# A two-layer encoder trunk on one core: attention's values one unit behind its scores, its products spread evenly, and loads and weights brought a stage forward

## The chip, the cores and the metric

The kernel runs on one core of a Trainium2 chip. The metric is the device time of one execution in microseconds, from the launch's first to its last instruction; lower is better. The core's engines run their own instruction streams and meet at semaphores: TensorE (PE, matmul; PEld is its weight load), VectorE (DVE), ScalarE (ACT), GpSimd (POOL) and SyncE (SP), which issues all DMAs of this kernel.

## What is computed

`encoder_trunk` is applied with the same weights to a prompt of 2048 rows and a sample of 512 rows, 1024 wide, all in float32. It has two layers; the first is the one that the change touches:

```python
h = rmsnorm(x, ln_g[0])
q_lat, kv_lat, k_pe, q_mem, gate = split(h @ w_in_a)          # 384, 256, 32, 256, 1024
q = rmsnorm((rmsnorm(q_lat) @ w_uq).reshape(S, 12, 96));  q = rope(q)
k_nope, v = split((rmsnorm(kv_lat) @ w_ukv).reshape(S, 12, 128))
k = rope(rmsnorm(concat(k_nope, k_pe)))                       # 12 heads of 96
o_mix = softmax(q @ k.T * 96 ** -0.5) @ v                     # prompt and sample each among themselves
x = x + (concat(o_mix, o_mem) * silu(gate)) @ w_out[0]        # o_mem: attention over 256 memory rows
```

The second layer has a spatial gating unit in attention's place.

## The kernel before

Rows are handled as 20 tiles of 128 (16 of the prompt, 4 of the sample). Every matmul operand is split into a high and a low part (`hi`, `lo`) in TensorE's reduced float32 form, and each product is three matmuls: hi x hi, hi x lo, lo x hi (lines 169 to 173). The high part is a copy by ScalarE, the low part a subtraction by VectorE. The stages run one after another, each in a block of its own. The exit of a space that owns semaphores (line 58) clears them and sets a barrier for all engines.

**Latents** (`latents`, line 312). Steps 0 to 20. A step normalizes and transposes the next row tile (`NormTranspose`: `square` on ScalarE, `root` on GpSimd, `scale` on VectorE, `turn` on TensorE, `round_hi`, `take_lo`), makes the 48 matmuls of the latents of this tile (`products`), and turns, splits and stores the latents of the tile before. In steps 2, 4, ... 16 a tile of memory rows is turned as well, in the middle of the products, its two halves at k = 2 and k = 5 (line 379). A turn waits until the low half of the transposition before has been taken. x tiles have two buffers. The order of each engine's work in a step is written out by hand (lines 354, 398, 433, 451, 491).

**Weights** (`Weights`, line 123, `Plan`, line 92). Raw weights go through a buffer of 6144 columns; ScalarE copies the high and VectorE subtracts the low part. A stage's first pieces are loaded by the stage before (`load_following`). The heads have five pieces, three of 1152 columns and two of 1536; four fit, and the fifth is loaded in the heads' stage.

**Heads** (`heads`, line 509). Per tile: queries (27 matmuls of 384 columns) and keys with values (18 of 512) from the latents, norms, rotary positions (tables made by GpSimd at the start, lines 753 to 769), transpositions of keys two tiles behind (`turn_k`) and of queries one tile behind (`turn_q`), splits and stores to `qT`, `kT`, `vS`. SP's order per step is written at lines 592 to 604: values, keys of two tiles behind, latents two ahead, queries of one behind. The stage waits for all stores before it ends. On VectorE `value_lo` stands before the three `low_k` (lines 881 to 884).

**Attention** (`attention`, line 955). 12 heads x 5 chunks of 512 queries: parts 0 to 3 of the prompt with 8 units of 256 keys each, and the sample with 2. A unit is: `scores` (6 matmuls of 512 columns into one of two PSUM buffers), two exponentials by ScalarE (lines 1203, 1204; the first is the high part of the probabilities), the low part by VectorE (line 1311), `value` (4 matmuls). GpSimd adds up the high parts (line 1277), so that the row sums need no matmul: per chunk 7 additions, then `fold`, `total_lo` and, of the outputs, `join`. `total` (2 matmuls) brings the sums into `o_lo`. The maximum over the keys is taken 22 pieces ahead: `maximum` (2 matmuls a unit), a reduction of each piece by VectorE (line 1297), and behind a chunk's last piece the reduction to one value per row and its negation `neg` (line 1305). This falls behind the fifth unit (t = 4) of parts 0, 1 and 2 and behind the seventh (t = 6) of parts 2 and 3. Four small DMAs (`row`, line 1048) write it as the bias row of the queries, for which the first scores of the next chunk wait. Scores of unit t + 1 wait for the low part of unit t - 1. TensorE's order is:

```python
for t in range(c.pairs):
    if t < c.pairs - 1:
        scores(c, t + 1)
    maximum(*max_pieces(c, t))
    if nxt.exists() and t == c.pairs - 1:
        scores(nxt, 0)
    if t == 0 and has_before(c):
        finish_values(prev)          # the last two units of the chunk before
    if t >= 2:
        value(c, t - 2)
    if t == 3 and has_before(c):
        total(prev)
```

GpSimd's order in a chunk of 8 is fold (of the chunk before), additions 1 and 2, total_lo, addition 3, join, additions 4 to 7. At the stage's start SP loads queries 0, keys 0, queries 1 and values 0; VectorE sets the constant rows (lines 1318 to 1322), for which `maximum` waits too; then come 22 pieces of maxima and the first scores.

After attention come `gate_memory`, `gated_output`, and `spatial` with the same two for layer 1 (`build`, line 2211).

## Time and profile before

| | us |
|---|---|
| median of 3 runs (3455.32 to 3460.83) | 3456.26 |
| the profiled execution | 3457.05 |
| its span, first to last instruction | 3455.3 |
| PE busy | 3244.4 (94%) |
| PE weight loads busy | 2752.9 (80%) |
| DVE busy | 2024.7 (59%) |
| ACT busy | 1707.5 (49%) |
| POOL busy | 1398.5 (40%) |

The profile is of one execution; times count from the span's start. The granted clock is a share of full speed (1.00 is 2.4 GHz, 0.50 is 1.2 GHz); its mean over the span is 0.969. "busy" is the time in which at least one instruction of the engine runs; matmuls are pipelined and overlap in the records (one of 512 columns lasts 0.39 to 0.40 us and the next starts 0.23 us later), so a TensorE that is 99% busy need not be at its peak: the distance of the starts shows it. In a timeline row the first number is the start, the second the duration, "xN" the number of merged instructions, and the bracket the idle time of the engine before them and who ended it. In a row of waits stand who waited for whom, then us in total, times, and the longest.

### The profile page before, as it was taken

What the parts mean: (1) busy time and instruction counts of PE and PEld (TensorE: products, weight loads), DVE (VectorE), ACT (ScalarE), POOL (GpSimd) and SP (SyncE); (2) the same over time, 40 slices, a digit from 0 to 9 for tenths busy, and PEclk for the clock granted to TensorE, in tenths of its full rate; (3) what the DMA queues carried; (4) which work ended last, traced back from release to release, by engine and by line L of the source; (5) the groups of instructions that cost most, each with busy time, mean ns of one, the idle gap of its engine ahead of it and who ended that gap; (6) DMA issues with size and microseconds to landing.
All of it is one profiled execution on the core that took longest, in us unless ns stands there. A gap on an engine that the chain in (4) does not pass through costs nothing. (4 is left out here: it accounts for less than half of the span.)

```text
span 3455.3 us, 46901 instructions
## 1 busy us (share of the span) xinstructions
PE 3244.4 (94%) x17548; PEld 2752.9 (80%) x17548; DVE 2024.7 (59%) x2857; ACT 1707.5 (49%) x2472; POOL 1398.5 (40%) x910
## 2 busy tenths in 40 slices
PE   7979979999999999999979997998999979999899
PEld 6978856777777777777769997786788869999787
DVE  4548878888888888888753333444333234333432
ACT  4436645777777777777744544102222225444200
POOL 1228856888888888888910000000110000000000
PEclk9989979999999999999989998998999989999999
DMA  7858983333213333321053233885323233322565
GB/s 285 307 211 311 328 281 73 63 68 64 50 41 63 68 65 68 64 59 36 11 200 110 89 111 89 243 229 185 140 97 108 81 144 126 107 91 85 165 192 157
DMA packets 380229, 454.75 MB, mean 132 GB/s; under 512 B 51704, under 2 KB 317304, under 8 KB 367728
## 3 DMA queue, kind: packets, MB, share of 16 engines
q1 hardware_dynamic: 380016, 451.91, 42.5%
q8 instruction: 134, 2.20, 0.3%
q14 instruction: 79, 0.65, 0.1%
HBM read 262.07 MB, written 189.64 MB: 131 GB/s over the span
## 5 line engine op out<-in xcount | busy, mean ns | idle before, releaser
L1277 POOL TENSOR_TENSOR at_acc<-at_acc,at_ph 128x1024 f32<-128x1024 f32 x288 | 690.6, 2398 | 76.1 <-ACT at_ph L1203 55.7
L1203 ACT ACTIVATE at_ph<-at_sc 128x1024 fp32r<-128x1024 f32 x408 | 418.5, 1026 | 322.8 <-PE at_sc L1123 322.8
L1311 DVE TENSOR_TENSOR at_pl<-at_sc,at_ph 128x1024 fp32r<-128x1024 f32 x408 | 498.5, 1222 | 129.7 <-ACT at_sc L1204 129.3
L1297 DVE TENSOR_REDUCE at_mx<-at_mxp 128x1 f32<-128x512 f32 x816 | 522.1, 681 | 25.8 <-PE at_mxp L1134 23.8
L1204 ACT ACTIVATE at_sc<-at_sc 128x1024 f32<-128x1024 f32 x408 | 416.0, 1020 | 0.0
L171 PE MATMUL gm_gate<-gm_h,gm_g_hi 128*128 128x256 f32 x1280 | 367.7, 287 | 6.4 <-DVE gm_g_lo L160 6.4
L172 PE MATMUL gm_gate<-gm_h,gm_g_hi 128*128 128x256 f32 x1280 | 362.1, 283 | 0.0
L173 PE MATMUL gm_gate<-gm_h,gm_g_lo 128*128 128x256 f32 x1280 | 361.9, 283 | 0.0
L1119 PE MATMUL at_sc<-at_qt,at_kt 97*128 97x512 f32 x816 | 330.5, 405 | 3.9 <-DVE at_pl L1311 1.9
L1121 PE MATMUL at_sc<-at_qt,at_kt 96*128 96x512 f32 x816 | 325.0, 398 | 0.0
L1148 PE MATMUL at_o_hi<-at_ph,at_v 128*128 128x512 f32 x816 | 322.3, 395 | 2.1 <-DVE at_half L1316 2.1
L1123 PE MATMUL at_sc<-at_qt,at_kt 96*128 96x512 f32 x816 | 322.5, 395 | 0.0
L1150 PE MATMUL at_o_lo<-at_pl,at_v 128*97 128x512 f32 x816 | 321.9, 395 | 0.0
L1134 PE MATMUL at_mxp<-at_kt,at_qt 96*128 96x512 f32 x816 | 275.7, 410 | 22.7 <-DMA at_kt<-kT 17.9
L171 PE MATMUL ou_acc<-ou_o_hi,ou_og 128*128 128x512 f32 x640 | 252.4, 394 | 43.1 <-DVE ou_o_lo L160 35.3
L1632 POOL TENSOR_TENSOR gm_rstd<-gm_mean,all_mhalf 128x4 f32<-128x4 f32 x40 | 40.3, 1007 | 618.7 <-DVE gm_mean L1772 618.7
L172 PE MATMUL ou_acc<-ou_o_lo,ou_og 128*128 128x512 f32 x640 | 251.6, 393 | 0.0
L173 PE MATMUL ou_acc<-ou_o_hi,ou_og 128*128 128x512 f32 x640 | 251.2, 393 | 0.0
L171 PEld LDWEIGHTS gm_gate<-gm_h,gm_g_hi 128*128 128x128 f32 x1280 | 245.1, 192 | 6.8 <-DVE gm_g_lo L160 6.8
L172 PEld LDWEIGHTS gm_gate<-gm_h,gm_g_hi 128*128 128x128 f32 x1280 | 245.6, 192 | 0.0
L173 PEld LDWEIGHTS gm_gate<-gm_h,gm_g_lo 128*128 128x128 f32 x1280 | 245.3, 192 | 0.0
L1919 ACT CAST ou_og<-ou_full 128x1024 fp32r<-128x1024 f32 x40 | 42.0, 1049 | 392.2 <-DVE ou_full L1938 392.2
(240 smaller groups left out, 7297.1 us busy)
## 6 DMA issues: line engine op xcount, KB each, us to landing
gm_h<-hT SPq DMA_DIRECT2D x48, 1024.0 KB, 7.2
hT<-lat_n_h SPq DMA_DIRECT2D x28, 1024.0 KB, 7.2
qT<-hd_stq SPq DMA_DIRECT2D x60, 384.0 KB, 5.4
kT<-hd_stk SPq DMA_DIRECT2D x60, 384.0 KB, 4.7
at_qt<-qT SPq DMA_DIRECT2D x120, 192.0 KB, 3.0
sgT<-gm_sg SPq DMA_DIRECT2D x80, 256.0 KB, 2.1
ou_o<-omix SPq DMA_DIRECT2D x40, 512.0 KB, 6.3
ou_sg<-sgT SPq DMA_DIRECT2D x40, 512.0 KB, 7.4
```

The source lines that it names most:

```text
L171: pe.matmul(out, a_hi, w_hi, start=first, stop=False)
L172: pe.matmul(out, a_hi, w_lo, start=False, stop=False)
L173: return pe.matmul(out, a_lo, w_hi, start=False, stop=last)
L1119: pe.matmul(sc[g][:, b, :], kt[:, c.kv, 0, ks], qt[:, c.quad, 0, :], start=True, stop=False)
L1121: pe.matmul(sc[g][:, b, :], kt[0:QK, c.kv, 0, ks], qt[0:QK, c.quad, 1, :], start=False, stop=False)
L1123: m = pe.matmul(sc[g][:, b, :], kt[0:QK, c.kv, 1, ks], qt[0:QK, c.quad, 0, :], start=False, stop=True)
L1148: pe.matmul(o_hi[:], v[:, c.kv, n, 0:2 * VH], ph[:, g, b, :], start=first and b == 0, stop=last and b == 1)
L1203: act.activation(ph[:, g], sc[g % 2][:], ACT.Exp, scale=SCALE).then_inc(p_hi, 1)
L1204: act.activation(sc[g % 2][:], sc[g % 2][:], ACT.Exp, scale=SCALE).then_inc(p_in, 1)
L1277: pool.tensor_tensor(acc[:, c.slot, :], f32(ph[:, (g - 1) % 4]).rearrange("p b n -> p (b n)") if t == 1 else acc[:, c.slot, :], now, ALU.a ...
L1297: dve.tensor_reduce(mx[:, n:n + 1], mxp[n % 2][:], AX.X, ALU.max).then_inc(mx_in, 1)
L1311: dve.tensor_tensor(pl[:, g], sc[g % 2][:], f32(ph[:, g]), ALU.subtract).then_inc(p_lo, 1)
```

## The change

It moves work between stages and changes orders; what is computed stays the same.

- Attention, TensorE: every unit is now scores, maximum, values; the first scores of the next chunk stand ahead of the last maxima. Values run one unit behind; the last unit's values of a chunk follow in the next chunk's first step, values 0 and 1 both at t = 2. `total` moves from t = 3 to t = 1 (t = 2 behind a sample chunk), starts the accumulation in `o_lo`, and waits for the copy `low` of the chunk before.
- Attention, ScalarE: `total_hi` one or two steps earlier, before exponentials 1; `low` is copied before `up`. GpSimd: `total_lo` before addition 1 (before addition 2 behind a sample chunk).
- Latents: only the first gains are loaded first, the others after tile 0; the turns of the memory tile move from k = 2 and 5 to k = 3 and 6; ScalarE rounds before it squares; in steps 2 to 6 one piece of the heads' weights is split per step; the fifth piece is loaded in step 5, the following stage's six in step 13, the first two latent tiles in step 16.
- Heads: all weights are there at the start; the first low key part is taken before the values'; in the drain, between the stores of the last queries and of the last keys, queries 0, keys 0 (16 tiles) and queries 1 of attention are loaded, and the sample's keys 0 after the waits for all stores.
- `build`: the spaces for the above, with semaphores of their own. The keys' buffer is split into two tensors, so the constants have one more instruction.

```diff
+        self.gains_in = [s.sem(f"n_gains{n}") for n in range(2)]
...
-    def load_gains(self, sp):
-        for tile, rows in zip(self.g, self.gains):
-            sp.dma_start(tile[:], rows.broadcast_to([P, D])).then_inc(self.g_in, 16)
+    def load_gains(self, sp, others):
+        for n in range(1, len(self.g)) if others else (0,):
+            sp.dma_start(self.g[n][:], self.gains[n].broadcast_to([P, D])).then_inc(self.gains_in[others], 16)
...
+        if self.order[n][2] > 0:
+            dve.wait_ge(self.gains_in[1], 16 * (len(self.gains) - 1))
...
+class HeadsAhead:
+
+
+    STEPS = 5
+
+    def __init__(self, s, plan, following):
+        self.w = Weights(s, plan, following)
+        self.lat = s.sb("lat", [P, 2, 2, QL + KVL], F32R)
+        self.lat_in = [s.sem(f"lat{u}") for u in range(2)]
+
+    def load(self, sp, u, rows):
+        sp.dma_start(f32(self.lat[:, u]), rows).then_inc(self.lat_in[u], 16)
+
+
+class KeysAhead:
+
+
+    def __init__(self, s):
+        self.k0 = s.sb("k0", [QK + 1, 2, TOK], F32R)
+        self.q = s.sb("q", [QK + 1, 4, 2, BLK], F32R)
+        self.q_load = [s.sem(f"q_load{u}") for u in range(4)]
+        self.kh_load = [s.sem(f"kh_load{u}") for u in range(2)]
+        self.kl_load = [s.sem(f"kl_load{u}") for u in range(2)]
+
+    def load_q(self, sp, qT, head, part, quad):
+        for a in range(2):
+            sp.dma_start(f32(self.q[0:QK, quad, a]).rearrange("d (t n) -> d t n", n=P),
+                         qT[part * 4:(part + 1) * 4, head // 4, :, head % 4, a].rearrange("t d n -> d t n")
+                         ).then_inc(self.q_load[quad], 16)
+
+    def load_first(self, sp, kT, a, b):
+
+        for n, sem in ((0, self.kh_load[0]), (1, self.kl_load[0])):
+            sp.dma_start(f32(self.k0[0:QK, n, a * P:b * P]).rearrange("d (t n) -> d t n", n=P),
+                         kT[a:b, 0, 0:QK, n, 0].rearrange("t p n -> p t n")).then_inc(sem, 16)
...
+                norm.load_gains(sp, 1)
                 w.load(sp)
 
                 def step(i):
+                    if i == 5:
+                        ahead.w.load_rest(sp)
+                    if i == 13:
+                        ahead.w.load_following(sp)
...
+                    if i == 16:
+                        for u in range(2):
+                            sp.wait_ge(stored[u], 16)
+                            ahead.load(sp, u, latT[u])
...
-                        if beside and k in (2, 5):
-                            norm.turn(pe, beside[0], k // 5)
+                        if beside and k in (3, 6):
+                            norm.turn(pe, beside[0], k // 6)
...
+                    turned = list(norm.between(i, i + 1))
+                    for n in turned[:1]:
+                        for half in range(2):
+                            norm.round_hi(act, n, half)
                     for n in norm.between(i + 1, i + 2):
                         norm.square(act, n)
-                    for n in norm.between(i, i + 1):
+                    for n in turned[1:]:
                         for half in range(2):
                             norm.round_hi(act, n, half)
                     if here(i):
                         square(i)
                     if here(i - 1):
                         round_hi(i - 1)
+                    if 2 <= i < 2 + ahead.STEPS:
+                        ahead.w.round_hi(act, i - 2, i - 1)
 
...
+                    if 2 <= i < 2 + ahead.STEPS:
+                        ahead.w.take_lo(dve, i - 2, i - 1)
...
-        w = Weights(s, plan, following)
-        lat = s.sb("lat", [P, 2, 2, QL + KVL], F32R)
+        w, lat, lat_in = ahead.w, ahead.lat, ahead.lat_in
...
-                load_lat(Tile(0, 0))
...
-                load_lat(Tile(0, 1))
-                w.load(sp)
...
+                    if t.known and t.n == TILES:
+                        sp.wait_ge(q_st[0], 16 * PT_TILES)
+                        keys.load_q(sp, qT, 0, 0, 0)
+                        sp.wait_ge(k_st[0], 16 * PT_TILES)
+                        keys.load_first(sp, kT, 0, PT_TILES)
+                        keys.load_q(sp, qT, 0, 1, 1)
...
+                keys.load_first(sp, kT, PT_TILES, TILES)
 
             @block.tensor
             def _(pe):
+                w.ready(pe, "ukv", 1)
...
                         key_mean(t1)
+                    if t2.within(TILES):
+                        low_k(t2, 0)
+                    if t1.within(TILES):
                         value_lo(t1)
                     if t2.within(TILES):
-                        for c in range(G):
-                            low_k(t2, c)
+                        low_k(t2, 1)
+                        low_k(t2, 2)
...
-        kt = s.sb("kt", [QK + 1, 2, 2, TOK], F32R)
-        qt = s.sb("qt", [QK + 1, 4, 2, BLK], F32R)
+        kt, qt = (keys.k0, s.sb("k1", [QK + 1, 2, TOK], F32R)), keys.q
...
+            first = 16 if c.head % 2 == 0 and c.n > 0 else 0
+            return first + 16 * sum(len(list(key_pieces(n))) for n in range(c.head % 2, c.head + 1, 2))
...
+        def total_at(c):
+
+            return 2 if before(c, 1).sample else 1
...
                 c0 = Chunk(0)
-                load_q(c0)
-                load_k(0)
-                load_q(c0.ahead(1))
                 load_v(0)
-                sp.wait_ge(const_in, 5)
+                sp.wait_ge(const_in, 6)
                 row(c0)
...
-                        if c.part == 0:
+                        if c.part == 0 or c.n == Chunk.PARTS - 1:
                             pe.wait_ge(kl_load[c.kv], keys_loaded(c))
...
-                                      start=first and b == 0, stop=last and b == 1)
+                                      start=first and b == 0 and not has_before(c), stop=last and b == 1)
                     m.then_inc(valued, 1)
 
                 def total(c, alone=False):
 
                     pe.wait_ge(tot_lo_in, c.n + 1)
+                    pe.wait_ge(low_in, c.n + 1)
                     for n, part in enumerate((tot_hi, tot_lo)):
                         m = pe.matmul(o_lo[0:ROW_HI + 1, :], pick[:, 0:ROW_HI + 1], part[:, c.slot, :],
-                                      start=alone and n == 0, stop=alone and n == 1)
+                                      start=n == 0, stop=alone and n == 1)
                     m.then_inc(tot_mm, 1)
...
-                    value(c, c.pairs - 2)
-                    if c.pairs == 2 and has_before(c):
-                        total(before(c, 1))
-                    value(c, c.pairs - 1)
+                    for t in range(0 if c.sample else c.pairs - 1, c.pairs):
+                        value(c, t)
 
                 def step(c):
                     nxt, prev = c.ahead(1), before(c, 1)
                     for t in range(c.pairs):
                         if t < c.pairs - 1:
                             scores(c, t + 1)
+                        elif nxt.exists():
+                            scores(nxt, 0)
                         maximum(*max_pieces(c, t))
-                        if nxt.exists() and t == c.pairs - 1:
-                            scores(nxt, 0)
                         if t == 0 and has_before(c):
                             finish_values(prev)
-                        if t >= 2:
-                            value(c, t - 2)
-                        if t == 3 and has_before(c):
+                        if has_before(c) and t == total_at(c):
                             total(prev)
+                        if not c.sample and t == 2:
+                            value(c, 0)
+                        if not c.sample and t >= 2:
+                            value(c, t - 1)
 
                 run_chunks(pe, step)
                 last = Chunk(Chunk.COUNT - 1)
                 finish_values(last)
-                pe.wait_ge(low_in, last.n + 1)
                 total(last, alone=True)
...
-                    act.copy(up[:], o_hi[VH:2 * VH, :]).then_inc(up_in, 1)
                     if c.n >= 2:
                         act.wait_ge(o_out[c.slot], stored(c))
                         act.wait_ge(o_in, c.n - 1)
                     act.copy(low[:, c.slot, :], o_lo[0:ROW_HI + 1, :]).then_inc(low_in, 1)
+                    act.copy(up[:], o_hi[VH:2 * VH, :]).then_inc(up_in, 1)
...
-                        if has_before(c) and t == (2 if c.pairs == 8 else 1):
+                        if has_before(c) and t == total_at(c) - 1:
                             total_hi(prev)
...
                         if t == 0 and has_before(c):
                             fold(prev)
+                        if has_before(c) and t == total_at(c):
+                            total_lo(prev)
                         if t > 0:
...
-                        if has_before(c) and t == (2 if c.pairs == 8 else 1):
-                            total_lo(prev)
                         if has_before(c) and t == (3 if c.pairs == 8 else 1):
                             join(prev)
...
-                dve.memset(f32(kt[QK:QK + 1, :, 0, :]), 1.0).then_inc(const_in, 1)
+                for u in range(2):
+                    dve.memset(f32(kt[u][QK:QK + 1, 0, :]), 1.0).then_inc(const_in, 1)
...
+        with ExitStack() as early, Space(nc, "ka", side="right") as s3:
+            s2 = early.enter_context(Space(nc, "ha"))
             kpe_all = s2.sb("kpe", [P, TILES, RP])
-            latents(nc, K, A, *next(steps), rows(A["x"], True),
-                    [A["ln_g"][0:1, :], A["mem_norm_g"][0:1, :], A["mem_norm_g"][1:2, :]], hT, latT, kpe_all)
-            heads(nc, K, A, *next(steps), latT, kpe_all, qT, kT, vS)
-        attention(nc, K, qT, kT, vS, omix, sums)
+            lat_plans, head_plans = next(steps), next(steps)
+            ahead = HeadsAhead(s2, *head_plans)
+            latents(nc, K, A, *lat_plans, rows(A["x"], True),
+                    [A["ln_g"][0:1, :], A["mem_norm_g"][0:1, :], A["mem_norm_g"][1:2, :]], hT, latT, kpe_all, ahead)
+            keys = KeysAhead(s3)
+            heads(nc, K, A, ahead, keys, latT, kpe_all, qT, kT, vS)
+            early.close()
+            attention(nc, K, keys, qT, kT, vS, omix, sums)
```

## Rows read from the trace of the kernel before

**Rows 1.** Busy us by engine with counts, clock, DMA share, GB/s: heads' loop, attention

```profile
265.20:485.00 219.80, 212.23 (x1224) 186.12 (x1224) 179.79 (x244) 141.11 (x207) 183.59 (x131) 1.00 0.88 318
535.00:1730.00 1195.00, 1186.31 (x4978) 908.04 (x4978) 1044.00 (x1379) 884.58 (x991) 1054.21 (x526) 1.00 0.26 56
```

**Rows 2.** Attention, PE: third unit; second maximum; weight loads, waits from 600

```profile
1010.78 0.40 PE L1150 MATMUL at_o_lo<-at_pl,at_v 128*97 128x512 f32 x1
1011.21 0.50 PE L1119 MATMUL at_sc<-at_qt,at_kt 97*128 97x512 f32 x1
1023.43 0.19 PEld L1134 LDWEIGHTS at_mxp<-at_kt,at_qt 96*128 96x128 f32 x1 [0.35 <-DVE at_mx L1297]
PEld at_mxp L1134 <- DVE at_mx L1297: 22.3, 76, 0.4
```

**Rows 3.** Attention, a chunk inside: timeline around a negation (L1305)

```profile
992.73 1.03 ACT L1203 ACTIVATE at_ph<-at_sc 128x1024 fp32r<-128x1024 f32 x1 [1.33 <-PE at_sc L1123]
992.82 4.94 POOL L1277 TENSOR_TENSOR at_acc<-at_acc,at_ph 128x1024 f32<-128x1024 f32 x2
994.49 0.74 DVE L1305 TENSOR_SCALAR at_neg<-at_m 128x4 fp32r<-128x4 f32 x1
995.15 1.21 DVE L1311 TENSOR_TENSOR at_pl<-at_sc,at_ph 128x1024 fp32r<-128x1024 f32 x1
996.71 0.40 PE L1119 MATMUL at_sc<-at_qt,at_kt 97*128 97x512 f32 x1
L1305 DVE TENSOR_SCALAR at_neg<-at_m x60: 170/744/1680, 525.4 to 1698.9; 128x4 fp32r<-128x4 f32 x60
```

**Rows 4.** Attention, first chunk: timeline around its negation

```profile
545.55 1.03 ACT L1203 ACTIVATE at_ph<-at_sc 128x1024 fp32r<-128x1024 f32 x1 [0.84 <-PE at_sc L1123]
546.65 2.39 POOL L1277 TENSOR_TENSOR at_acc<-at_acc,at_ph 128x1024 f32<-128x1024 f32 x1 [0.39 <-ACT at_ph L1203]
547.39 1.68 DVE L1305 TENSOR_SCALAR at_neg<-at_m 128x4 fp32r<-128x4 f32 x1
549.30 0.40 PE L1150 MATMUL at_o_lo<-at_pl,at_v 128*97 128x512 f32 x1
550.25 0.50 PE L1119 MATMUL at_sc<-at_qt,at_kt 97*128 97x512 f32 x1 [0.56 <-DVE at_pl L1311]
```

**Rows 5.** Attention, POOL at a chunk's start: first addition, total's low part

```profile
1005.35 2.40 POOL L1277 TENSOR_TENSOR at_acc<-at_ph 128x1024 f32<-128x1024 f32 x1 [1.17 <-ACT at_ph L1203]
1011.42 1.28 POOL L1253 TENSOR_TENSOR at_tot_lo<-at_tot,at_tot_hi 128x512 fp32r<-128x512 f32 x1
```

**Rows 6.** Latents: PE's waits; VectorE's subtraction for the heads' weights (heads' start)

```profile
PE lat_n_pt L283 <- DVE lat_n_h L299: 9.6, 8, 1.3
L160 DVE TENSOR_TENSOR hd_uq_lo<-all_w_raw,hd_uq_hi 128x1152 fp32r<-128x1152 f32 x3 | 3.9, 1353 | 5.3 <-ACT hd_uq_hi L155 5.3
```

**Rows 7.** Heads: start of tables, TensorE's restart; PE's waits in the loop

```profile
244.45 1.53 POOL L754 TENSOR_TENSOR hd_tmpa<-hd_cosq,hd_graw 128x640 f32<-128x640 f32 x1 [20.75 <-DMA hd_graw<-in_g_rope]
265.17 0.47 PE L171 MATMUL hd_pkv<-hd_ukv_hi,hd_lat 128*128 128x512 f32 x1 [1.79 <-DVE hd_vst L832]
PE hd_pt L626 <- DVE hd_stk L827: 3.9, 13, 0.4
```

**Rows 8.** Heads to attention: SP, constants, first maximum; DMA from 504; SP's waits

```profile
504.41 7.96 SPq L1032 DMA_DIRECT2D at_qt<-qT  x2
508.15 0.06 DVE L1322 MEMSET at_pick<- 128x1 f32 x1
512.05 1.19 PE L1134 MATMUL at_mxp<-at_kt,at_qt 96*128 96x512 f32 x2 [17.92 <-DMA at_kt<-kT]
504.00:512.00 8.00, 0.00 (x0) 0.00 (x0) 3.90 (x5) 0.00 (x0) 0.00 (x0) 0.50 1.12 194
SPq L61 <- PEq L61: 0.6, 1, 0.6
```

**Rows 9.** DMA issues from 480 to 545: KB each, median us to landing

```profile
at_qt<-at_neg SPq DMA_DIRECT2D x4, 0.5 KB, 2.0
```

More of the change, by code:

```diff
@@ L398, in step @@
                 def step(i):
-                    ahead = list(norm.between(i, i + 1))
-                    if ahead:
+                    nexts = list(norm.between(i, i + 1))
+                    for n in nexts[:1]:
                         for half in range(2):
-                            norm.turn(pe, ahead[0], half)
+                            norm.turn(pe, n, half)
                     if here(i):
-                        products(i, ahead[1:])
+                        products(i, nexts[1:])
                     if here(i - 1):
@@ L467, in _ @@
             def _(dve):
[L468 removed]
+                dve.wait_ge(norm.gains_in[0], 16)
                 norm.scale(dve, 0)
@@ L987, in attention @@
              "o_in"))
-        q_load = [s.sem(f"q_load{u}") for u in range(4)]
-        kh_load = [s.sem(f"kh_load{u}") for u in range(2)]
-        kl_load = [s.sem(f"kl_load{u}") for u in range(2)]
+        q_load, kh_load, kl_load = keys.q_load, keys.kh_load, keys.kl_load
         v_load = [s.sem(f"v_load{u}") for u in range(2)]
@@ L1006, in keys_loaded @@
         def keys_loaded(c):
-            return 16 * sum(len(list(key_pieces(n))) for n in range(c.head % 2, c.head + 1, 2))
+            first = 16 if c.head % 2 == 0 and c.n > 0 else 0
+            return first + 16 * sum(len(list(key_pieces(n))) for n in range(c.head % 2, c.head + 1, 2))
         def stored(c):
@@ L1029, in load_q @@
                 def load_q(c):
-                    group, at = c.head // HPG, c.head % HPG
-                    for a in range(2):
-                        sp.dma_start(f32(qt[0:QK, c.quad, a]).rearrange("d (t n) -> d t n", n=P),
-                                     qT[c.part * QT:(c.part + 1) * QT, group, :, at, a].rearrange("t d n -> d t n")
-                                     ).then_inc(q_load[c.quad], 16)
+                    keys.load_q(sp, qT, c.head, c.part, c.quad)
                 def load_k(head):
```

53 lines of the change are left out of this document (22 added, 31 removed).

## The prediction

> **What bounds the kernel now.** I read the busy times by stage first, then what the engines wait for in each stage, then single stretches of the timeline. By stage [rows 1] TensorE is busy 97% of the heads' loop (220 us) and 99.3% of attention, which alone lasts 1195 us of the 3455.3 us span, and its clock is granted in full in both (1.00). So attention is TensorE's, and the question is what its busy time hides. In an undisturbed run a 512-column matmul starts every 0.23 us. There are two places per chunk where it doesn't [rows 2]. At 1010.78 to 1011.21 the step is 0.43 us, because scores of the next unit wait for VectorE's low halves, and the matmul after it is 0.10 us slower. And the second maximum at the chunk's end waits 0.35 us for VectorE (1023.43), because two pairs of maxima stand there with only four matmuls of values between. That is 0.20 + 0.11 + 0.34 = 0.65 us a chunk; the weight load of the maxima waits so 76 times in 1100 us, more than once in each of the 48 chunks of eight units, and I take the whole for 45 of them: 45 x 0.65 = 29.3 us. This is what even spacing can give back.
>
> VectorE and GpSimd stand close behind: 1044 and 1054 us of 1195 [rows 1]. They also hold each other up. The negated maximum (L1305) is a 128x4 operation; it takes 0.17 us at best, but 0.74 at the median and 1.68 at most over 60 times, and each long one ends together with GpSimd's operation beside it [rows 3]. At 994.49 it starts inside the addition that runs since 992.82, and ends at 995.23, when that ends (4.94 us for two, 2.4 each). At 547.39 it starts 0.74 us into an addition and ends at 549.07, 0.03 us after that one [rows 4]. The Trainium skill (SBUF — State Buffer, Who interferes with whom) says so as a rule: an operation such as tensor_scalar may enter a mode that needs the port pair shared with GpSimd, and the one that comes first holds it for its whole instruction. The trace agrees, with the two ends above.
>
> **The change, part by part.** The sum is made against the profiled execution, 3457.05 us (span 3455.3 and 1.75 around it); the median of the runs shown, 3456.26, is 0.8 below.
>
> Attention, spacing. Maxima, scores and values alternate evenly, and the values stand one unit behind. Scores of unit t+1 then have 18 matmuls (4.2 us) since the end of scores t-1, except 16 where the total stands; exponentials (2 x 1.03 [rows 4]) and subtraction (1.21 [rows 3]) plus 0.25 of starting need 3.5. Both waits go: -29.3.
>
> Attention, GpSimd's order. The low part of the total (1.28 us) now comes before the chunk's first addition instead of after the second. Before, GpSimd idled 1.17 us ahead of the first addition, and the total's low part then delayed all later ones [rows 5]. That delay has been useful. Call E the start of a unit's exponentials. Unhindered, an addition starts 1.10 us after E [rows 4] (545.55, 546.65). In rows 3 the addition that belongs to E = 992.73 starts only at 995.3, 1.5 us late, so the negation (E + 1.76) meets the end of the one before and costs nothing on TensorE: the scores at 996.71 start on time. Without the 1.28 us the lag is 0.2 or less; my step-by-step schedule of a full chunk gives 0.1. The addition then runs from E + 1.1 to E + 3.5, the negation falls into it and ends at E + 3.5, the subtraction at E + 4.7, and the scores, due at E + 4.0, wait. Rows 4 show this very case in the first chunk, where GpSimd had no total to form: scores at 550.25 instead of 549.53, and 0.12 us more on the next one, **0.84 us**. There are 60 negations, in every head three behind a chunk's fifth unit and two behind a seventh; the first comes before any unit, and the first chunk's is paid already. 58 x 0.84 = 48.7. In the chunk behind a sample chunk the total stays behind the first addition, so the lag there is about 0.35: still inside the addition, 11 x 0.35 = 3.9 more. Together +52.6. The bound below is nothing (no negation caught), above 58 x 1.4 = 81 (lag just short of 0.66). With the spacing: attention +23.3. The wait for the copied low sums, added ahead of the total, ends by the same schedule 0.5 us before TensorE comes to it; behind it the scores of the next unit would queue. Cost 0.
>
> Latents. TensorE waits 9.6 us in 8 places for the low half before the second transposition of a step [rows 6]; moving that six matmuls (0.91 us) later leaves 7 x 0.39: -6.9. The subtractions of the heads' weights stand at the end of steps 2 to 6, on VectorE's path to that wait where a memory tile follows, in two of them: 1.35 and, by width, 1.8: +3.1. Six loads of 512 KB (3.1 MB) go ahead of the x tiles in step 13; at 318 GB/s, what the heads' loop moves [rows 1], that is 9.8 us of queue. Only the first x tile behind them is urgent, and it is loaded a good half step ahead: I take a third, +3.5, bounds 0 and 9.8. The gains' later load frees the first tile earlier, but the second half of the weights then queues behind them: 0, bounds -3 and +2. The last six loads are in part those that the heads made at 252 us. Sum -0.3.
>
> Heads' start. Weights and two latent tiles are there, so the waits of 10 and 8 us go. What is late next is GpSimd's rotary tables: they begin at 244.45, when the gains' rows land, and their chain ends at TensorE's restart at 265.17 [rows 7]. Those small loads shared the queue with two latent tiles (0.66 MB each) and a weight tile (0.79 MB), which are gone from it. One tile ahead and one weight tile behind, 1.4 MB at 318 GB/s, are 4.4 us: the tables begin at 240, -4.4 (bounds -2.1, the tile ahead alone, and -6.6, all three).
>
> Heads' loop. The first low key half is taken before the values': the 13 waits of 3.9 us [rows 7] go: -3.9 (bound 0). The values' low half comes 0.56 us later, five microseconds before it is needed.
>
> Heads to attention. Queries 0, keys 0 (16 tiles) and queries 1, 2.4 MB, are issued between the stores of the last queries and of the last keys (L569 before them, L574 behind them). At 194 GB/s, what these loads reach [rows 8], that is 11.9 us of queue ahead of the last keys' stores, for which the stage waits before it ends, and 0.9 us for issuing the sample keys behind that wait. Attention's blocks start 12.8 us later. The loads no longer hold the maxima (512.05), but the constants do, ready at 508.21 of before: 521.0 instead of 512.05, **+9.0**. Bounds: +12.8, and -3.8 if the stores are not held. The spaces of what is brought forward have semaphores of their own, which are cleared, with a barrier, once before attention and once after it, where there was none; TensorE's side of such an exit shows as a wait of 0.6 us of SP's [rows 8]: 2 x 0.5 = +1.0, bounds 0 and 2. The Trainium skill (DMA: Bandwidth & Descriptors, Queues, rings and completion order) has descriptors of one issuer consumed in ring order on each engine; by it the sum is the +9.0, without it -3.8. The trace speaks for it: a load of queries behind the keys took 7.96 us to issue [rows 8].
>
> **Sum**: +23.3 - 0.3 - 4.4 - 3.9 + 9.0 + 1.0 = +24.7, so 3481.8, against the median 3481. Its own range: 3465 (the stores aren't held, and the heads gain all) to 3493 (half of the upper bounds).
>
> **Rivals.** First, **faster**: GpSimd stays more than 0.66 us behind. Then the negations meet the end of the addition before, as now [rows 3]. For it speaks that I reckon the lag only by adding durations, some ten in a row; against it, the 1.17 us of idling that the moved operation fills [rows 5]. It decides at a lag of 0.66 us at the fifth unit. Attention then gives -29.3 + 3 of small waits, total -25: 3431 against the median. Second, **in between**: only the fifth units' negations of two chunks are caught, 24 x 0.84 = 20, and the queue costs half: -29.3 + 20 - 8.6 + 5.5 = -12, or, with the chunks behind a sample caught too (11 x 1.2), about +1: 3444 to 3457. Third, **slower still**: the bias rows leave only when the negation has ended; four copies are issued some 0.6 us apart and land 2.0 us after issue [rows 9], so the last at E + 3.5 + 1.8 + 2.0 = E + 7.3, and the next chunk's first scores want them at E + 7.6. It decides from 0.3 us more on, and then each chunk pays: at 0.5 us, 48 x 0.5 = 24 more, 3505. Fourth, **the spacing doesn't do what it says**, because scores still wait for VectorE: 0.3 us of slack only where the total stands; at 0.3 a chunk it adds 14 us: 3495.
>
> **Chances.** A difference under 0.2% (7 us) can't be told from none here. Forecast 0.60, rival one 0.24, two 0.08, three and four 0.08. Slower comes out of the forecast, three and four: 0.67. Faster is rival one and a part of two: 0.27. Same: 0.06. The range of 8 in 10 must reach from rival one to the top of the forecast: 3427 to 3493.
>
> **What would show it.** L1305 at 1.6 us and ending with GpSimd's additions, 58 times; those starting 1.1 us after the exponentials; scores waiting 0.5 to 0.7 us for low halves behind the fifth and seventh unit; no wait of L1134 on maxima; a head's period of 102 us instead of 99.8. Ahead of it: the first maximum near 521 less the 8.6 us won before, near 512; last keys' stores landing some 12 us after the loads' issue; tables from 240. If L1305 stays at 0.74 us or less, and a head lasts 97.5 us, the forecast is wrong by its largest term.

## The result, and the profile after

The changed kernel took 3494.34 us, the median of 4 runs (3487.69 to 3496.71), beside 3456.11 before: a ratio of 1.0102, with a 95% interval of 1.0089 to 1.0114. It is slower, by 35 us by the ratio and 38 by the medians. The profiled execution spans 3492.7 us, 37.4 more than before.

Busy times by stretch come first (the columns are those of [rows 1]), then the negations (L1305 has become L1357) and TensorE's waits between 600 and 1700 us:

```profile
265.20:485.00 219.80, 212.36 (x1220) 187.42 (x1219) 178.11 (x247) 142.21 (x210) 180.70 (x132) 0.98 0.91 325
535.00:1730.00 1195.00, 1154.69 (x4876) 891.91 (x4876) 1097.43 (x1366) 868.65 (x967) 1028.56 (x511) 1.00 0.26 56
L1357 DVE TENSOR_SCALAR at_neg<-at_m x60: 170/1818/2103, 526.9 to 1729.9; 128x4 fp32r<-128x4 f32 x60
PE at_sc L1171 <- DVE at_pl L1363: 37.7, 54, 1.0
PEld at_mxp L1186 <- DVE at_mx L1349: 5.2, 33, 0.2
PEld at_sc L1171 <- DMA ka_q<-at_neg: 2.0, 10, 0.4
```

In the same 1195 us of attention TensorE starts 4876 matmuls where it started 4978, and is busy 32 us less, while VectorE is busy 53 us more, with 13 instructions fewer: it does not work more, it stands. The negation took 0.74 us at the median [rows 3] and takes 1.82. The waits of the maxima [rows 2] have gone from 22.3 to 5.2 us; the waits of the scores for the low halves (L1363, L1311 before) have come. One fifth unit in the timeline, then the same negation one head later:

```profile
1005.98 1.03 ACT L1255 ACTIVATE at_ph<-at_sc 128x1024 fp32r<-128x1024 f32 x1 [0.84 <-PE at_sc L1175]
1007.24 2.40 POOL L1331 TENSOR_TENSOR at_acc<-at_acc,at_ph 128x1024 f32<-128x1024 f32 x1
1007.62 0.17 DVE L1352 TENSOR_REDUCE at_m<-at_mx 128x4 f32<-128x16 f32 x1
1007.82 1.85 DVE L1357 TENSOR_SCALAR at_neg<-at_m 128x4 fp32r<-128x4 f32 x1
1009.58 1.21 DVE L1363 TENSOR_TENSOR at_pl<-at_sc,at_ph 128x1024 fp32r<-128x1024 f32 x1
1009.87 2.37 POOL L1331 TENSOR_TENSOR at_acc<-at_acc,at_ph 128x1024 f32<-128x1024 f32 x1 [0.23 <-ACT at_ph L1255]
1009.72 0.40 PE L1202 MATMUL at_o_lo<-at_pl,at_v 128*97 128x512 f32 x1
1010.85 0.50 PE L1171 MATMUL at_sc<-ka_q,ka_k 97*128 97x512 f32 x1 [0.73 <-DVE at_pl L1363]
1011.19 0.40 PE L1173 MATMUL at_sc<-ka_q,ka_k 96*128 96x512 f32 x1
1110.01 1.81 DVE L1357 TENSOR_SCALAR at_neg<-at_m 128x4 fp32r<-128x4 f32 x1
```

The reduction L1352, as small as the negation, takes 0.17 us while GpSimd's addition runs (1007.24 to 1009.64); the negation right behind it takes 1.85 and ends when that addition does, 0.20 us ahead of the next one (1009.87). Such an instruction is called held below. The scores' first matmul starts 1.13 us after the last of the values instead of 0.23, and the next is 0.11 late: 1.01 us. Five such stalls stand in the head from 1007.82 to 1110.01: 1.01, 0.83, 0.84, 1.19 and 0.93 us. That head lasts 102.19 us.

By stage, from the same events in both traces (us):

| stretch, and the event that ends it | before | after | difference | forecast |
|---|---|---|---|---|
| latents, the last turn | 225.62 | 225.06 | -0.6 | -0.3 |
| heads' start, TensorE's restart | 265.17 | 258.49 | -6.1 | -4.4 |
| heads' loop, the last turn that waits for VectorE | 492.22 | 483.69 | -1.9 | -3.9 |
| to the first maximum | 512.05 | 513.46 | +9.9 | +9.5 |
| attention, the last sums' store | 1736.13 | 1769.24 | +31.7 | +23.3 |
| to the next stage's first load | 1738.78 | 1772.91 | +1.0 | +0.5 |
| the rest, the end | 3455.3 | 3492.7 | +3.3 | 0 |

The last line is in part scatter: this stretch, in which the two kernels do the same, took 1715.7 to 1720.6 us in the twelve profiled executions of this study. The rows of the middle, in their order, each to be read beside [rows 6 to 8]:

```profile
172.87 0.47 PE L286 MATMUL lat_n_pt<-all_ident,lat_n_xs 128*128 128x128 f32 x1 [5.43 <-DVE lat_n_h L302]
239.17 1.57 POOL L809 TENSOR_TENSOR hd_tmpa<-hd_cosq,hd_graw 128x640 f32<-128x640 f32 x1 [16.03 <-DMA hd_graw<-in_g_rope]
245.39 1.57 POOL L816 TENSOR_TENSOR hd_krope<-ha_kpe,hd_tmpa 128x640 f32<-128x640 f32 x1
258.49 0.76 PE L171 MATMUL hd_pkv<-ha_ukv_hi,ha_lat 128*128 128x512 f32 x1 [10.11 <-DVE hd_vst L886]
484.48 2.35 SPq L341 DMA_DIRECT2D ka_q<-qT  x2
486.88 2.60 SPq L348 DMA_DIRECT2D ka_k<-kT  x2
489.52 5.83 SPq L341 DMA_DIRECT2D ka_q<-qT  x2
495.39 2.08 SPq L629 DMA_DIRECT2D kT<-hd_stk  x3
503.94 0.87 SPq L348 DMA_DIRECT2D ka_k<-kT  x2
513.33 0.06 DVE L1375 MEMSET at_pick<- 128x1 f32 x1
513.46 0.80 PE L1186 MATMUL at_mxp<-ka_k,ka_q 96*128 96x512 f32 x1 [27.86 <-DVE at_pick L1375]
```

GpSimd's tables start at 239.17 instead of 244.45. SP spends 10.87 us (484.48 to 495.35) on issuing the loads of queries and keys, and only then issues the last keys' stores (L629). The first maximum waits for the constants, no longer for keys.

### The profile page after: what moved, and what is told of

Read it like the earlier page. It is cut to its first block and busy times, and to the rows that moved or that the text cites. A ratio compares the mean times of both kernels' runs of the same rounds, so it can differ in the third digit from the quotient of the medians.

```text
span 3492.7 us, 46990 instructions
## 1 busy us (share of the span) xinstructions
PE 3237.7 (93%) x17548; PEld 2757.4 (79%) x17548; DVE 2088.7 (60%) x2858; ACT 1714.5 (49%) x2472; POOL 1403.3 (40%) x910
## 5 line engine op out<-in xcount | busy, mean ns | idle before, releaser
L1363 DVE TENSOR_TENSOR at_pl<-at_sc,at_ph 128x1024 fp32r<-128x1024 f32 x408 | 497.4, 1219 | 87.7 <-ACT at_sc L1256 83.7
L1349 DVE TENSOR_REDUCE at_mx<-at_mxp 128x1 f32<-128x512 f32 x816 | 521.2, 679 | 26.7 <-PE at_mxp L1186 26.6
L171 PE MATMUL sg_acc<-sg_uv_hi,sg_n_h 128*128 128x512 f32 x480 | 193.0, 402 | 7.1 <-ACT sg_v L2166 6.4
L1200 PEld LDWEIGHTS at_o_hi<-at_ph,at_v 128*128 128x128 f32 x816 | 153.6, 188 | 47.5 <-issue 1.0
L172 PE MATMUL sg_acc<-sg_uv_lo,sg_n_h 128*128 128x512 f32 x480 | 190.0, 396 | 0.0
L173 PE MATMUL sg_acc<-sg_uv_hi,sg_n_h 128*128 128x512 f32 x480 | 190.0, 396 | 0.0
```

Of the source, the lines that this page charges most:

```text
L171: pe.matmul(out, a_hi, w_hi, start=first, stop=False)
L172: pe.matmul(out, a_hi, w_lo, start=False, stop=False)
L173: return pe.matmul(out, a_lo, w_hi, start=False, stop=last)
L1200: pe.matmul(o_hi[:], v[:, c.kv, n, 0:2 * VH], ph[:, g, b, :], start=first and b == 0, stop=last and b == 1)
L1349: dve.tensor_reduce(mx[:, n:n + 1], mxp[n % 2][:], AX.X, ALU.max).then_inc(mx_in, 1)
L1363: dve.tensor_tensor(pl[:, g], sc[g % 2][:], f32(ph[:, g]), ALU.subtract).then_inc(p_lo, 1)
```

## The experiments

All ran beside the kernel before (medians of it 3455.7 to 3458.1 us).

**1. The form of the negation.**

```diff
-dve.tensor_scalar(neg[:, c.slot, :], m4[:], -1.0, None, ALU.mult).then_inc(neg_in, 1)
+dve.tensor_reduce(neg[:, c.slot, :], m4[:].rearrange("p (q n) -> p q n", n=1), AX.X, ALU.max,
+                  negate=True).then_inc(neg_in, 1)
```

> The changed kernel, with the negation of the four maxima written as a reduction over one element with its sign turned (128x4, same place, same waits) instead of a tensor_scalar; the reduction just ahead of it (L1352, same size) takes 0.17 us in the middle of a GpSimd addition. Theory (the negation is held until GpSimd's addition ends, 58 stalls of 0.95 us): it takes 0.17 to 0.2 us, the 57 waits of the scores (L1171) for the low halves are gone, a head lasts about 97.6 us instead of 102.4, the time falls by 50 to 58 us, to about 3440. Rival (whatever stands there on VectorE is late, because the values one unit behind leave no slack): the waits stay and the time is above 3485.

Measured: 3438.35 us, ratio 0.9943 (0.9926 to 0.9960), 56.0 less than the changed kernel (55 by the two ratios). Now the row of the negations, and TensorE's stretch:

```profile
L1357 DVE TENSOR_REDUCE at_neg<-at_m x60: 157/157/159, 530.6 to 1676.4; 128x4 fp32r<-128x4 f32 x60
600.00:1700.00 1100.00, 1099.50 (x4713) 864.90 (x4712) 969.95 (x1305) 842.39 (x938) 998.85 (x497) 1.00 0.27 57
PEld at_sc L1171 <- DVE at_pl L1364: 1.6, 4, 0.5
```

0.157 to 0.159 us, 60 times. From the first scores to the last sums' store attention lasts 1179.9 us, 58.2 less than in the changed kernel (1238.1) and 26.6 less than before (1206.5); ten heads in the middle last 97.4 us each at the mean (from a head's first scores to the next one's), where they last 102.3 in the changed kernel and 99.8 before. The 56 us are the form of one 128x4 instruction.

**2. Which forms are held, and what the holding costs.** In one kernel the negation is a product of two tiles in SBUF; in the other it is the reduction, and the tensor_scalar stands behind it and writes a spare tile.

```diff
+        minus = s.sb("minus", [P, 4])
...
-dve.tensor_scalar(neg[:, c.slot, :], m4[:], -1.0, None, ALU.mult).then_inc(neg_in, 1)
+dve.tensor_tensor(neg[:, c.slot, :], m4[:], minus[:], ALU.mult).then_inc(neg_in, 1)
...
```

```diff
+        spare = s.sb("spare", [P, 4])
...
-dve.tensor_scalar(neg[:, c.slot, :], m4[:], -1.0, None, ALU.mult).then_inc(neg_in, 1)
+dve.tensor_reduce(neg[:, c.slot, :], m4[:].rearrange("p (q n) -> p q n", n=1), AX.X, ALU.max,
+                  negate=True).then_inc(neg_in, 1)
+dve.wait_ge(neg_in, c.n + 1)
+dve.tensor_scalar(spare[:], m4[:], -1.0, None, ALU.mult)
```

> The changed kernel, with the negation as a tensor_tensor product with a constant tile of -1 (128x4, all operands in SBUF), same place. Theory A (every elementwise form whose operands all lie in SBUF is held): 1.8 us at the median, time about 3494. Theory B (only forms with one tensor operand are held, a tensor_tensor isn't): 0.2 us, time about 3439.

> The changed kernel with the negation as a reduction, and behind it, into a spare tile that nobody reads, the old tensor_scalar of the same size. The bias rows are early, only VectorE's later work stands behind the tensor_scalar. Theory (what costs is that VectorE is held and the subtraction queues behind it, whatever the result is for): tensor_scalar at 1.6 to 1.9 us, 57 waits of the scores for low halves, time 3492 to 3500. Rival (the late bias row costs): about 3440.

Measured: 3496.5 and 3492.3 us (2 runs each; ratios 1.0115, 1.0069 to 1.0160, and 1.0102, 1.0072 to 1.0133). The product's durations in the first kernel:

```profile
L1358 DVE TENSOR_TENSOR at_neg<-at_m,at_minus x60: 162/1830/2096, 526.1 to 1728.2; 128x4 fp32r<-128x4 f32 x60
```

In the second kernel, the negation, the spare tensor_scalar and the scores' waits:

```profile
L1358 DVE TENSOR_REDUCE at_neg<-at_m x60: 157/157/161, 530.1 to 1731.5; 128x4 fp32r<-128x4 f32 x60
L1361 DVE TENSOR_SCALAR at_spare<-at_m x60: 170/1626/1941, 530.3 to 1731.7; 128x4 f32<-128x4 f32 x60
PE at_sc L1172 <- DVE at_pl L1367: 37.6, 54, 1.0
```

Theory A holds: a tensor_tensor with both inputs in SBUF is held like the tensor_scalar. The subtraction L1363, which reads one operand from PSUM, is not: 1.22 us while additions run. And in the second kernel the result is early (0.157 us) and nobody wants what the tensor_scalar writes, yet the whole loss is there. So it is the queue on VectorE that costs, not the bias row. The Trainium skill (SBUF — State Buffer, Who interferes with whom) draws the line in the same place: on this chip tensor_reduce never contends with GpSimd, tensor_scalar may, and a tensor_tensor does when both its inputs lie in SBUF. The three medians here, 0.157, 1.63 and 1.83 us, agree.

**3. The total back in its old place**, in chunks of eight units: its two matmuls at t = 3, its low part behind the second addition. The spacing of scores, maxima and values stays as changed.

```diff
-            return 2 if before(c, 1).sample else 1
+            return 1 if c.sample else 3
...
+                        if has_before(c) and not c.sample and t == 2:
+                            total_lo(prev)               # GpSimd, behind addition 2
...
```

> The changed kernel, with the total alone back in its old place in chunks of eight units: GpSimd's total_lo behind the second addition, total_hi behind the third exponentials, the total's two matmuls at t = 3. The spacing of scores, maxima and values stays. Theory (the 1.28 us of total_lo behind the second addition make GpSimd late, so that the negation meets the end of the addition before): the negations behind the fifth unit take 0.8 us or less at the median, the waits of the scores for low halves fall from 57 to under 15, the time falls by 40 to 55 us, to about 3445. Rival (GpSimd's lag doesn't depend on that place): negations stay at 1.8 us, time above 3480.

Measured: 3477.75 us, ratio 1.0058 (1.0041 to 1.0075), 16.6 less than the changed kernel where 40 to 55 were expected. The row of the negations, and one behind a fifth and one behind a seventh unit:

```profile
L1363 DVE TENSOR_SCALAR at_neg<-at_m x60: 170/171/2254, 526.5 to 1713.2; 128x4 fp32r<-128x4 f32 x60
1078.24 0.17 DVE L1363 TENSOR_SCALAR at_neg<-at_m 128x4 fp32r<-128x4 f32 x1
1107.24 1.95 DVE L1363 TENSOR_SCALAR at_neg<-at_m 128x4 fp32r<-128x4 f32 x1
```

Behind the fifth units it is as expected: 0.17 us, three times a head. Behind the seventh units the negation is still held, for 1.90 to 2.25 us, two times a head. In the kernel before these too were short (0.18 and 0.17 us at 1000.13 and 1023.61), with the total in the same place; so by the seventh unit GpSimd's lag depends as well on what is left of the new order in attention, of which the spacing is the main part. A head lasts 100.82 us: over the 97.2 that its 418 matmuls take one every 0.2325 us two stalls of about 1.1 each, and, in three chunks, 0.30 and 0.15 near the chunk's start (scores and values that wait for VectorE at 1014.02 and 1016.14), where the total's two matmuls no longer stand between. The theory stands for three of five negations and falls for two.

**4. The negation behind the subtraction**, its form unchanged.

```diff
                         low_of(c, t)
+                        negate()              # what maxima() left of it in the unit before
...
```

> The changed kernel, with the tensor_scalar kept as it is, but behind the next unit's subtraction (L1363) instead of ahead of it. Theory: it is still caught by the addition that runs, but starts at E + 3.2 and ends with it at E + 3.6 (E is the start of the unit's exponentials), so about 0.5 us each; the subtraction is no longer behind it, the waits of the scores are gone, and the time falls by 50 to 55, to about 3441. Rival (the bias row is then too late for the next chunk's first scores): waits of L1171 for the bias DMAs of 0.5 us a chunk or more, and 20 us given back.

Measured: 3480.95 us, ratio 1.0064 (1.0047 to 1.0081), 13.4 less. The negations, and TensorE's waits for the bias rows from 600 to 1700:

```profile
L1366 DVE TENSOR_SCALAR at_neg<-at_m x60: 172/564/851, 528.2 to 1720.3; 128x4 fp32r<-128x4 f32 x60
PE at_sc L1171 <- DMA ka_q<-at_neg: 29.4, 44, 1.1
```

The theory is right on the instruction (0.56 us) and on the subtraction (no wait for low halves is left), and the rival decides the time: the row leaves no earlier than in the changed kernel (3.5 to 4.0 us after the start of the unit's exponentials in both, 2.0 in experiment 1), since it ends with the same addition, and TensorE, no longer late by its stall, waits for it 44 times, 0.67 us each. One stall had covered the other.

**5. The kernel before with the reduction.**

> The kernel before, with only the form of the negation changed to a reduction over one element. Theory (in the kernel before the delay of GpSimd lets the negation meet the end of an addition, so nearly nothing is lost): negations 0.17 us, and the time falls by 0 to 4 us. Rival (the form is worth tens of microseconds in any order): falls by more than 15.

Measured: 3456.1 us (10 runs), ratio 1.0001 (0.9992 to 1.0011): nothing. In that order the negations that are held (0.74 us at the median) stand on no path that TensorE waits for.

**6. Attention's orders all as before, the rest of the change kept.**

> The changed kernel, with every order inside attention as before (TensorE, ScalarE, GpSimd), so that what is left are the changes of latents, heads, the loads brought forward and the spaces. Theory (these sum to +1 to +4 us: latents -0.6, heads -8, heads to attention +10, spaces +1): 3457 to 3460, with attention's heads at 99.8 us. Rival (part of the loss in attention comes from the spaces or the keys' buffer in two tensors, not from the order): above 3465.

Measured: 3465.45 us (10 runs), ratio 1.0021 (1.0011 to 1.0031), so 3461 to 3468 by the interval, above the 3457 to 3460 of the theory and at the edge of the rival. Its profile is 7.7 longer than before's: first maximum +2.7, attention +3.0, exit +1.1, rest +0.9. Ten heads in the middle last 99.95 us each where they last 99.82 before, so the spaces and the split buffer cost at most 1.3 us in attention's rhythm. Of the other 1.7 us of attention 1.2 stand in the first head, where the clock came back later (below), and 0.5 at the end. Against this kernel the new order, with the negation freed (experiment 1), is worth 1209.5 - 1179.9 = 29.6 us of the stage, of which some 1.3 are again the clock in the first head; between experiments 5 and 1 it is 1204.7 - 1179.9 = 24.8.

**7. The loads back in attention.**

```diff
-                    if t.known and t.n == TILES:
-                        sp.wait_ge(q_st[0], 16 * PT_TILES)
-                        keys.load_q(sp, qT, 0, 0, 0)
...
                 c0 = Chunk(0)
+                keys.load_q(sp, qT, 0, 0, 0)
+                keys.load_first(sp, kT, 0, TILES)
+                keys.load_q(sp, qT, 0, 1, 1)
                 load_v(0)
...
```

> The changed kernel, with the loads of queries 0, keys 0 and queries 1 back at the start of attention, so that nothing stands ahead of the last keys' stores. Theory (2.4 MB ahead of the last stores hold the end of the heads' stage back, and the constants wait for that): attention's first instruction comes 11 to 13 us earlier, the loads land after the constants, the first maximum at 503 to 505 us instead of 513.5, the time falls by 8 to 10, to about 3485. Rival (the stage's end is held by its own stores and barriers, not by the loads): the first maximum stays above 511 and the time is within 3 us of the changed kernel's.

Measured: 3478.84 us, ratio 1.0060 (1.0043 to 1.0077), 15.5 less than the changed kernel. In its timeline, SP's stores and first load, the last constant and the first maximum:

```profile
485.05 3.16 SPq L629 DMA_DIRECT2D kT<-hd_stk  x3
493.32 0.88 SPq L341 DMA_DIRECT2D ka_q<-qT  x2
500.42 0.06 DVE L1370 MEMSET at_pick<- 128x1 f32 x1
502.35 1.19 PE L1181 MATMUL at_mxp<-ka_k,ka_q 96*128 96x512 f32 x2 [16.38 <-DMA ka_k<-kT]
```

The last keys' stores are issued from 485.05 instead of 495.39, the constants are there at 500.48 and the keys bind again, at 502.35: 11.1 us earlier. Once issued they also land sooner, 4.3 to 4.9 us after their issue instead of 6.5 to 6.9, so that the last of them is there at 491.81 instead of 503.86. Of the 15.5 us the other 4 are not explained by this edit; between the two profiles attention differs by 1.6 us and the stretch behind it, equal in both, by 4.1.

**8. Both repairs, and the weights' loads later.** The first kernel joins 1 and 7; the second moves, besides, the following stage's six loads:

```diff
-                    if i == 13:
+                    if i == 18:
                         ahead.w.load_following(sp)
```

> The changed kernel with both: the negation as a reduction, and the loads of queries 0, keys 0 and queries 1 back in attention. Theory (two separate costs that add up): 56 + 12 less than the changed kernel, about 3426, faster than both kernels. Rival (one hides the other, or the earlier start collides with the loads of head 1): above 3435.

> As the kernel with reduction and loads in attention, and the six loads of 512 KB of the following stage go in step 18 of the latents instead of 13. Theory (the 5.4 us wait of the changed kernel at 172.87 is an x tile queued behind them): this wait falls to 0.4 and the time by 4 to 5, to about 3421. Rival (they then stand ahead of the stores at the stage's end, or of the rotary tables' rows): nothing gained, the tables start 4 us later.

Measured: 3425.24 us, ratio 0.9910 (0.9893 to 0.9927), and 3415.43 us, ratio 0.9881 (0.9864 to 0.9897). The first is 69.1 below the changed kernel, where the parts give 56.0 + 15.5 = 71.5: they add up within 2.4. The second gains 9.8 more where 4 to 5 were expected. The waits of a step's second transposition in the latents, in the first kernel:

```profile
PE lat_n_pt L286 <- DVE lat_n_h L302: 14.0, 9, 5.6
173.28 1.11 PE L286 MATMUL lat_n_pt<-all_ident,lat_n_xs 128*128 128x128 f32 x4 [5.58 <-DVE lat_n_h L302]
```

And in the second:

```profile
PE lat_n_pt L286 <- DVE lat_n_h L302: 7.3, 8, 2.1
```

The wait of 5.58 us is gone, and with it what followed it. In the changed kernel, whose wait there is 5.43 us, the clock fell:

```profile
170.00:175.00 5.00, 2.13 (x9) 2.13 (x10) 2.84 (x4) 1.06 (x3) 0.74 (x2) 0.76 0.86 288
175.00:180.00 5.00, 5.00 (x35) 5.00 (x35) 1.46 (x4) 3.16 (x9) 0.90 (x2) 0.90 1.01 421
```

so that step 13's loads cost the wait and, with 0.76 and 0.90 of the clock over 5 us each (0.50 from 172.59 to 176.00), 1.6 us of slower matmuls. In the first kernel of this pair the clock stayed at 0.50 until 179.17, about 3 us of slower matmuls, which with the wait is most of the 9.8. From the turn at 164.07 to the latents' end the changed kernel takes 60.99 us, this one 53.85 (162.56 to 216.41): 7.1 us. The second kernel beats both the kernel before and the changed one, by 41 and 79 us.

## Why the prediction was right, and where its numbers were off

Slower was forecast, with 0.67, at 3481 in 3427 to 3493; by the ratio it is 3491.5, just inside the top, and the plain median of the four runs, 3494.34, lies 1.3 us above that top. The mechanism is the forecast's, and its largest term was nearly exact.

- **Negations held by GpSimd, +52.6.** Shown. 59 of 60 are held, 1.5 to 2.1 us; taking the form away gives 56.0 us. The five stalls of a head are 0.97 us at the mean, forecast 0.84, and 1.19 in the chunk behind a sample, where 0.84 + 0.35 was forecast. The mean without that one is 0.91. So rival one (the lag stays over 0.66 us) and rival two (two chunks only) are out.
- **What makes GpSimd late.** I gave the whole of it to the total's place. Experiment 3 shows that for the fifth units; behind the seventh the rest of the new order suffices to bring GpSimd back in time (presumably the even spacing; no run has it apart from the other orders). That step of the argument was incomplete, and that it cost nothing here is luck: both edits came together.
- **Spacing, -29.3.** Shown in the rhythm: a head of 97.4 us in experiment 1 instead of 99.8 before, 2.4 us in each of twelve, 29. Over the whole stage it is 24.8 to 29.6 us by the kernel that it is held against (experiment 6): the new order loses about 1 us at the stage's end, and the clock at its start differs. Rival four falls with it.
- **The bias rows (rival three).** In the changed kernel 2.0 us of weight loads' waits in 1100 us: it did not decide. Experiment 4 shows that it lay right behind: with the stall gone and the negation as late, it takes 29.4 us.
- **Attention as a whole, +31.7 for +23.3.** Ten heads in the middle are 24.3 us longer (102.26 instead of 99.82 each), the first is 2.0 longer, and the last with the stage's end 5.3. In the first about 1.3 us are the clock, which came back 10 us after the first scores: in both kernels of experiment 2 and in experiment 7, which have the same stalls but the clock back after 4 to 5 us, this head lasts 102.0 us instead of 103.3. The copied low sums, which I costed at nothing, do hold the total once, in the very last chunk, where no next scores stand between:

```profile
1759.24 0.44 PE L1211 MATMUL at_o_lo<-at_tot_hi,at_pick 128*97 128x512 f32 x1 [3.46 <-ACT at_low L1267]
```

  Before, the last values waited 2.07 us near there for VectorE's halves; from the last scores to the last store it is now 14.8 us instead of 13.4.
- **Latents, -0.3, came out at -0.6, but by other parts.** The turns gained as forecast (1.30 to 0.40 us, for 7 x 0.9), the weights' splitting cost 2.9 (two waits of 1.66 and 2.07 us instead of 0.40) for 3.1. Step 13's loads cost 7.1, not 3.5: mis-sized, since I took a third of their queue, and left out the clock, which fell behind the wait of 5 us here. What gave it back is a term that I did not have. The gains' later load, costed at nothing, is worth nothing: the first turn starts at 9.59 instead of 13.07, but then TensorE waits for the second half of the weights until 26.01 (26.28 before), and at the third turn it is 0.45 us behind. At the next one, for x, it is 4.0 ahead (41.26 for 45.22). In the kernel before, ScalarE squared a memory tile ahead of rounding the transposed x tile, and that square waited for its load; the scaling of the next x tile stood behind both. In the changed kernel the rounding comes first. The kernel before, then the changed one:

```profile
41.63 1.06 ACT L258 ACTIVATE lat_n_junk<-lat_n_x 128x1024 f32<-128x1024 f32 x1 [9.29 <-DMA lat_n_x<-in_mem]
42.69 1.05 ACT L293 CAST lat_n_h<-lat_n_pt 128x512 fp32r<-128x512 f32 x2
45.22 1.97 PE L283 MATMUL lat_n_pt<-all_ident,lat_n_xs 128*128 128x128 f32 x8 [4.25 <-DVE lat_n_xs L274]
```

```profile
26.01 0.69 PE L171 MATMUL lat_acc<-lat_wq_hi,lat_n_h 128*128 128x384 f32 x1 [4.84 <-DVE lat_wkv_lo L160]
32.99 1.19 ACT L296 CAST lat_n_h<-lat_n_pt 128x512 fp32r<-128x512 f32 x2 [0.53 <-PE lat_n_pt L286]
```

  Past the first memory tile the lead is 4.3 us (53.48 for 57.79), and -4.3 - 6.3 + 2.9 + 7.1 = -0.6. This is read from the two traces; no run has ScalarE's order alone.
- **Heads' start, -4.4: -6.1.** Counted from the span's start the tables come 5.3 us earlier, for 4.4, and the restart 6.7. The 1.4 between them is a term I did not have: the addition at 245.39 takes 1.57 us where it took 3.05 before, when VectorE's subtraction of a weight, both inputs in SBUF, ran beside it (249.25 to 252.19, itself 2.94 us where the one at 237.01, of the same size with GpSimd idle, took 1.75). The times fit the same holding, seen from GpSimd's side; no run has it alone.
- **Heads' loop, -3.9: -1.9.** The 13 waits for the low key half are gone; VectorE's low half of the values, now later, makes the products wait instead, 1.1 us in 6 times. That leaves 2.8; what took the other 0.9 stays open.
- **Heads to attention, +9.0 and the spaces' +1.0.** +9.9 and +1.0 measured, the first with half of the spaces' term in it, and experiment 7 takes 11.1 off. The term is right in size and not quite in place: of the 12.05 us by which the last keys' stores land later than in experiment 7 (11.9 forecast) about 10 pass before they are issued, because SP's own issue of the loads took 10.87 us, and only some 2 in the queue. The Trainium skill's ring order (DMA: Bandwidth & Descriptors, Queues, rings and completion order), on which I leaned for +9.0 against -3.8, agrees with the landings (the loads by 501.09, the stores behind them from 502.03), but no run here tests it alone.
- **The top of the range.** The profile lies 12.7 us above the sum: 8.4 of it attention, 3.3 the stretch that I had left at 0, and 1.0 what is left of the other stages' errors, which largely cancel.

## What to carry to other kernels

Before an instruction is moved on GpSimd or VectorE, ask what falls into what: a VectorE instruction with two inputs in SBUF, or a tensor_scalar there, costs its own 0.17 us or the rest of GpSimd's instruction, and which of the two is set by the phase between the engines. Such small ones are best written as a reduction, which never waited here (60 of 60). An idle gap that a reordering fills may have been what kept two engines out of step, and a stall that is removed may only uncover the next wait: look in the trace for what ends just behind it. And a load issued early is paid by whatever its issuer has to issue next.

## What the runs showed of the hardware

- At one size the holding goes by the form: a 128x4 instruction of 0.16 to 0.17 us took up to 2.1 us as tensor_scalar or as tensor_tensor from SBUF (2.25 in experiment 3), and 0.157 to 0.161 in 60 of 60 as a reduction.
- After attention's idle start the granted clock stays at 0.50 for a time that differs between executions: it was back at 1.00 5 us after the first scores in the kernel before, 10 us after them in the changed kernel and in experiment 6, 4 to 5 in experiments 1, 5 and 7, and 13 in experiment 4 and in the second kernel of experiment 8. Between the two kernels of experiment 8, whose attention is the same, the first head lasts 97.5 us with the clock back after 4 us and 100.1 with it back after 13: a spread of 2.6 us that no edit explains. The stretch behind the first scores in the kernel before:

```profile
535.00:538.00 3.00, 2.57 (x10) 1.45 (x9) 3.00 (x4) 2.35 (x3) 1.88 (x1) 1.00 1.19 220
```

In the changed kernel:

```profile
535.00:538.00 3.00, 3.00 (x8) 1.92 (x8) 1.95 (x3) 2.38 (x4) 0.26 (x1) 0.50 1.18 239
538.00:541.00 3.00, 3.00 (x9) 2.35 (x8) 1.97 (x3) 1.28 (x2) 2.12 (x1) 0.50 1.18 207
541.00:545.00 4.00, 4.00 (x18) 3.16 (x17) 3.75 (x6) 3.17 (x4) 3.46 (x2) 0.97 1.18 293
```

- Issuing behind large transfers costs the issuer: two loads of 192 KB took SP 5.83 us to issue behind the keys' two of 768 KB, where two in front of them took 2.35.
